# Weighted sum of gathered expert rows: from one token per partition on the full array to eight tokens per gather on column tiles

## The chip, the cores and the metric

One core of one Trainium2 chip runs the whole program. The metric is the device time of one execution in microseconds (us). PE is the matmul engine (PEld its weight loads), DVE, ACT and POOL are the vector, scalar and GpSimd engines, SP issues the plain DMAs. POOL issues the indirect DMAs, called gathers here.

## The reference, cut to what matters

Two layers (shared shape, own weights) run over a prompt block of 128 tokens and a sample of 512. Each layer is a mixer (three kinds of heads) and then PEER, a retrieval of experts, in which nearly all bytes are moved. For each block of 128 tokens and each of 8 heads:

```python
s = einsum('nhpk,pmk->nhpm', q, sub_keys)              # 2 x 128 scores
sv, si = top_k(s, 16)                                  # on each half
cand = sv[:, :, 0, :, None] + sv[:, :, 1, None, :]     # 16 x 16
top_s, top_j = top_k(cand, 16);  e = expert numbers of top_j
g = softmax(top_s)
act = gelu(einsum('nd,nhkd->nhk', x, u[e]))
y = einsum('nhk,nhkd->nd', g * act, v[e])
x = x + gate * y
```

u and v have 16384 rows of 1024 floats per layer. Per block, 8 heads x 16 picks x 128 tokens rows of u and as many of v are fetched, 4 KB each. All is float32.

## The kernel before, in words

A *unit* is one head of one block of one layer: 2 x 5 x 8 = 80 units (`UNITS`), with 16 *rows* each. Row r of u is one gather: pick number r % 16 of all 128 tokens, partition p getting the expert row of token p (512 KB). Rows of v are fetched in the same way, from the same index tile `idx_st`. There are 1280 rows of each (`ALL_ROWS`).

All engines run one list of steps in the order of `whole_order`; each takes the steps that concern it, in order, and waits on semaphores. `weave` puts mixer steps between the row steps, in proportion to rough costs, and never right after the last row of a unit. Up to row 980 (of 1280) there is mixer work between most rows; after that there are only row steps. At step r:

- POOL (`expert_row`) issues v row r - 16 into one of four v buffers, once the sum of the row four before has ended (`summed`), and then u row r + 4 into one of four u buffers, once DVE has finished u row r.
- DVE multiplies u row r with the tokens and sums it to one column of `dots` (L1863), and does one piece of the top-k of the unit two ahead (`topk`, a generator). When a unit's 16 dots are there, DVE and ACT turn them into weights (`gelu_args`, `gelu`, `weights`), 128 x 16.
- ACT makes, for v row r - 18, a diagonal 128 x 128 matrix of its weights (`diagonal`, L1376, seven buffers).
- PE sums v row r - 20 (`V_LAG`): two matmuls, left and right half, diagonal x row, accumulated in `acc` (expert_sum in the trace) over the 128 rows of a block (L2200). In the trace each of these matmuls is two records, as is every float32 matmul of the kernel; a row is four.

After a block ACT copies the sum out, DVE gates it and adds it to x (`finish`). In the last 20 rows DVE adds every second v row itself (`add_row`, `SHARED_ROWS`), and the last 16 v rows also use the four u buffers, which are free then (`v_place`).

`work` is four PSUM banks for everything else on PE; `Banks` hands them out along the plan, by `fills_of`. The scores of a unit are one matmul into such a bank (`peer_scores`), made at the last row of the unit three before.

## Time and profile before

| | |
|---|---|
| median of 3 runs | 4307.49 us (4300.9 to 4318.6) |
| span of the profiled execution | 4295.3 us, first to last instruction; what lies around it is not in the trace (12.2 us against the median) |
| PE busy | 82% of the span, mean granted clock 0.967 |
| DVE, POOL, ACT busy | 60%, 60%, 18% |
| bytes moved | 1521 MB, of which 1342 MB by gathers; mean 354 GB/s |
| L2200, the weighted sum, on PE | 5080 records, 2505.5 us busy |
| L1863, dot products, on DVE | 1280, 1557.0 us busy |
| L1079, gathers, on POOL | 2 x 1280, 1233.9 + 1219.9 us busy |
| L1376, diagonals, on ACT | 1270, 446.4 us busy |

The profile is one execution. Busy time is the time in which an engine has an instruction running; the DMA share is the mean busy share of the core's 16 DMA engines (it can come out a little over 1 in short stretches). [...] "Idle before, releaser" says how long an engine had nothing to do and what ended it, by semaphore events; "issue" is that no releaser was found, "remote" that it was none of this core's engines. Ends of matmuls are modelled.

### The profile page before, as it was taken

The page shows a single profiled execution, that of the slowest core. Times are in us where ns is not written, and L with a number is a line of the kernel's source. Part 1 is how long each engine was busy: PE and PEld are TensorE (multiplying, and loading weights), DVE is VectorE, ACT ScalarE, POOL GpSimd, SP SyncE. Part 2 cuts the span into 40 slices and gives each one's busy share as a digit, 9 for nine tenths or more (in the row PEclk, how much of TensorE's full clock was granted, in tenths as well). Part 3 has the DMA queues.
Part 4 walks back from the last instruction along what each step waited for, and adds up shares of the span by engine and source line. Part 5 has one row for each costly group of instructions (what it writes and reads, how often), then busy time and mean ns, then how long its engine had stood idle before and what let it go on. Part 6 is the DMA issues. An engine that isn't in the chain of part 4 may idle for free.

```text
span 4295.3 us, 37781 instructions
## 1 busy us (share of the span) xinstructions
PE 3531.0 (82%) x10578; PEld 1680.6 (39%) x10578; DVE 2580.9 (60%) x6691; ACT 759.0 (18%) x2324; POOL 2588.3 (60%) x2835
## 2 busy tenths in 40 slices
PE   7798999889887778887877999998888877777776
PEld 3444555444343233433422555543433422222222
DVE  2545567757665665656565555776766566666654
ACT  2112212212111121211111122221211111111110
POOL 1256456666665666766666654666666666666665
PEclk8999999999999999999999999999999999999999
DMA  7887999999999999999999899999999999999998
GB/s 278 317 288 265 339 362 358 365 387 379 348 365 382 380 355 348 349 351 370 383 379 373 296 331 338 368 358 375 385 346 370 362 368 374 367 370 372 370 370 327
DMA packets 461412, 1521.29 MB, mean 354 GB/s; under 512 B 47092, under 2 KB 67352, under 8 KB 460696
## 3 DMA queue, kind: packets, MB, share of 16 engines
q0 software_dynamic: 368640, 1342.34, 82.9%
q1 hardware_dynamic: 92156, 176.43, 11.3%
q8 instruction: 90, 1.47, 0.1%
q14 instruction: 114, 0.93, 0.1%
q10 hardware_dynamic: 412, 0.11, 0.0%
HBM read 1513.04 MB, written 5.67 MB: 354 GB/s over the span
## 4 chain that ended last, share of the span: by engine, by line
PE 37%; DMA 19%; issue 18%; POOL 18%; DVE 5%; another core or an unknown queue 3%; ACT 1%; SPq 0%; ACTq 0%; DVEq 0%; POOLq 0%
PE expert_sum L2200 20%; POOL expert_rows L1079 16%; DMA expert_rows<-in_peer_v,experts 14%; PE work L1959 4%; DMA expert_rows<-in_peer_u,experts 4%; PE work L2151 3%; PE work L2166 2%; DVE expert_rows L1863 2%; PE work L1905 2%; PE work L2095 2%; PE work L2122 1%; POOL stat_rstd L1029 1%; PE work L1934 1%; PE work L2051 1%
## 5 line engine op out<-in xcount | busy, mean ns | idle before, releaser
L2200 PE MATMUL expert_sum<-expert_rows,weight_diagonals 128*128 128x512 f32 x5080 | 2505.5, 623 | 588.9 <-DMA expert_rows<-in_peer_v,experts 446.8
L1863 DVE CUSTOM_DVE_ANT_0 expert_rows<-expert_rows,tokens 128x1024 f32<-128x1024 f32 x1280 | 1557.0, 1217 | 912.3 <-DMA expert_rows<-in_peer_u,experts 806.2
L1079 POOL DMA_INDIRECT expert_rows<-in_peer_v,experts x1280 | 1233.9, 964 | 1006.2 <-PE expert_sum L2200 566.9
L2200 PEld LDWEIGHTS expert_sum<-expert_rows,weight_diagonals 128*128 128x128 f32 x5080 | 912.8, 195 | 1848.4 <-issue 1676.7
L1079 POOL DMA_INDIRECT expert_rows<-in_peer_u,experts x1280 | 1219.9, 953 | 449.2 <-issue 358.4
L1376 ACT ACTIVATE weight_diagonals<-ident,expert_weights 128x128 f32<-128x128 f32 x1270 | 446.4, 392 | 568.7 <-PE expert_sum L2200 217.3
L1959 PE MATMUL work<-weight_ring,h_or_mixed 128*128 128x384 f32 (+3 forms) x768 | 237.3, 463 | 12.4 <-DMA weight_ring<-in_w_in 10.6
L1905 PE MATMUL work<-ident,scratch 128*128 128x128 f32 (+1 forms) x770 | 127.2, 289 | 97.9 <-DVE scratch L1479 32.1
L1959 PEld LDWEIGHTS work<-weight_ring,h_or_mixed 128*128 128x128 f32 x768 | 140.1, 193 | 115.3 <-issue 61.1
L1905 PEld LDWEIGHTS work<-ident,scratch 128*128 128x128 f32 (+1 forms) x770 | 97.7, 145 | 186.8 <-issue 86.1
L1315 ACT ACTIVATE scratch<-work,neg_max 128x640 f32<-128x640 f32 (+3 forms) x108 | 73.0, 676 | 502.2 <-DVE neg_max L1640 290.9
L1365 ACT ACTIVATE gelu_dots<-gelu_args 128x16 f32<-128x16 f32 x80 | 17.2, 216 | 809.1 <-issue 449.2
L2166 PEld LDWEIGHTS work<-h_or_mixed,weight_ring 128*128 128x128 f32 x1024 | 142.7, 194 | 37.8 <-issue 31.9
L2166 PE MATMUL work<-h_or_mixed,weight_ring 128*128 128x128 f32 (+1 forms) x1024 | 151.9, 304 | 4.9 <-DMA weight_ring<-in_peer_wq 3.8
L1026 POOL TENSOR_SCALAR stat_biased<-stat_sums 128x6 f32<-128x6 f32 (+1 forms) x82 | 17.5, 214 | 211.0 <-DVE stat_sums L1500 84.2
L1640 DVE TENSOR_REDUCE neg_max<-work 128x1 f32<-128x640 f32 (+3 forms) x120 | 76.3, 636 | 107.0 <-PE work L2095 67.9
L2151 PE MATMUL work<-weight_ring,scratch 128*128 128x512 f32 x304 | 133.6, 592 | 0.1
L1863 DVE DVE_READ_ACCUMULATOR2_ANT dots<- 128x1 f32 x1280 | 105.6, 82 | 0.0
L1500 DVE TENSOR_REDUCE stat_sums<-scratch 128x6 f32<-128x576 f32 (+1 forms) x42 | 27.6, 658 | 128.3 <-ACT scratch L1208 74.4
L1679 DVE COPY scratch<-work 128x512 f32<-128x512 f32 x20 | 13.8, 692 | 136.9 <-PE work L2151 136.9
L2151 PEld LDWEIGHTS work<-weight_ring,scratch 128*128 128x128 f32 x304 | 57.7, 190 | 73.1 <-issue 73.1
L1029 POOL TENSOR_TENSOR stat_rstd<-stat_biased,minus_half 128x6 f32<-128x6 f32 (+1 forms) x82 | 79.5, 969 | 6.8
(192 smaller groups left out, 2409.1 us busy)
## 6 DMA issues: line engine op xcount, KB each, us to landing
weight_ring<-in_w_mod SPq DMA_DIRECT2D x20, 2048.0 KB
weight_ring<-in_peer_wq SPq DMA_DIRECT2D x16, 2048.0 KB
weight_ring<-in_w_out SPq DMA_DIRECT2D x15, 2048.0 KB
expert_rows<-in_peer_u,experts POOLq DMA_INDIRECT x1280
expert_rows<-in_peer_v,experts POOLq DMA_INDIRECT x1280
weight_ring<-in_w_in SPq DMA_DIRECT2D x11, 1536.0 KB
expert_rows<-in_w_mod SPq DMA_DIRECT2D x4, 2048.0 KB, 13.7
weight_ring<-in_t_pool SPq DMA_DIRECT2D x4, 2048.0 KB
```

Of the source, the lines that this page charges most:

```text
L1029: g.tensor_tensor(stat_cols(rst, key, n), stat_cols(stp, key, n), half[:, 0:n], ALU.pow).then_inc(rstd_ready.sem, 1)
L1079: g.indirect_dma_start(buffer, None, table, bass.IndirectOffsetOnAxis(ap=idx_st[:, col:col + 1], axis=0),).then_inc(row_in, 16)
L1315: a_.activation(probs(item)[:, 0:n], src[:, 0:n], ACT.Exp, bias=nmax[:, i % 2:i % 2 + 1], accum_out=rsum[:, at:at + 1]).then_inc(banks.fre ...
L1376: a_.activation(diags[:, at * P:(at + 1) * P], ident[:, :], ACT.Copy, scale=wgt[:, col:col + 1]).then_inc(diag_ready, 1)
L1640: v_.tensor_reduce(nmax[:, i % 2:i % 2 + 1], s2[:, 0:n], AX.X, ALU.max, negate=True).then_inc(maxima.sem, 1)
L1863: v_.tensor_tensor_reduce(out=u_ring[r % U_RING], in0=u_ring[r % U_RING], in1=tokens[:, :], scale=1.0, scalar=0.0, op0=ALU.mult, op1=ALU.a ...
L1905: ins = t_.transpose(dst[0:n, j * P:(j + 1) * P], v, ident[:, :])
L1959: ins = t_.matmul(dst[:, lo:n], hT(b, kk), wt[:, kk, lo:n], start=kk == 0, stop=kk == KC - 1)
L2095: ins = t_.matmul(dst[:, col:col + m * P], lhs, tile(first, m)[lo:lo + n, :, pick, :], start=True, stop=True)
L2151: ins = t_.matmul(dst, o_T[:, kk, :], wt[:, kk, :], start=kk == 0, stop=kk == KC - 1)
L2166: ins = t_.matmul(dst[:, 0:len(blocks) * P], wt[:, kk, (h % 4) * P:(h % 4 + 1) * P], h_blocks[:, blocks[0]:blocks[-1] + 1, kk, :], start=k ...
L2200: ins = t_.matmul(acc[:, hf * 512:(hf + 1) * 512], diags[:, at * P:(at + 1) * P], v_buffer(row)[:, hf * 512:(hf + 1) * 512], start=first = ...
```

## The change

1. **What a v gather holds.** Partition p used to get pick k of token p. Now row k of a unit brings all 16 picks of eight tokens, those from 32 (k % 4) + 8 (k // 4) on: partition 16 i + m gets pick m of the i-th of them. For that the expert numbers of a unit have to be turned around between partitions: DVE spreads them into a masked 128 x 128 tile (`picked_of`), PE multiplies it with a 0/1 matrix (`of_group`) into 16 columns beside the scores of the unit two later, and DVE copies these to a new index tile `idx_v`.
2. **The weights.** The same turn for the weights: DVE makes the masked tile `pair_weights`, PE multiplies it with `of_group` at row 2 of the next unit (`pair_columns`), and DVE writes at row 3 (`SPREAD_AT`) the tile `spread` of 16 x 32 columns. ACT makes no diagonals any more.
3. **The sum.** The 16 gathers of a unit belong to 16 groups of eight tokens; four in turn (`STRIPS`) go to the four column tiles of 32. PE takes two gathers in one step, every second step, after both have landed: left half of the first, left half of the second, right half of the first, right half of the second. Each is a 128 x 32 weight against 128 x 512, and the two rows go to neighbouring column tiles. Each row counts up `summed` at its right half.
4. **Order.** `V_LAG` is 22 instead of 20: POOL issues v row r - 18 at step r, and PE sums rows r - 22 and r - 21 at even r. `weave` puts no mixer step after row 2 of a unit either. The DVE part in the last 20 rows is gone. Two more rounds of `peer_scores` follow at the end, for the turned numbers alone.
5. **Space.** The tile of the prompt's pooling matrix moves into another one and is loaded again for the second layer.

```diff
-U_RING, V_RING, DIAGS = 4, 4, 7
-V_LAG, DIAG_LAG = 20, 18
-SHARED_ROWS = ((ALL_ROWS - 20, ALL_ROWS),)
+U_RING, V_RING = 4, 4
+V_LAG, SPREAD_AT = 22, 3
+GROUPS, IN_GROUP, STRIPS, STRIP_T = 16, 8, 4, 32
...
+        def by_place(ap):
+            return ap.rearrange("p (i k) -> p i k", i=IN_GROUP)
+        def each_place(ap):
+            return ap.unsqueeze(1).broadcast_to([P, IN_GROUP, TOPK])
+        own_place = in_group[:, :].unsqueeze(2).broadcast_to([P, IN_GROUP, TOPK])
...
 POOL, expert_row:
+                    if v % TOPK == 0:
+                        pool.wait_ge(*banks.freed(("score", v // TOPK + 2)))
                     if no:
-                        pool.wait_ge(*v_done(v_turns[i][no - 1]))
+                        pool.wait_ge(*summed.done(v_turns[i][no - 1]))
-                    gather(peer_v, v_buffer(v), v_fills(v), v)
+                    gather(peer_v, idx_v, v_buffer(v), v_fills(v), v)
...
 ACT, expert_row:
-                if 0 <= r - DIAG_LAG < ALL_ROWS and not added_by_dve(r - DIAG_LAG):
-                    diagonal(r - DIAG_LAG)
...
 DVE, topk:
+                if unit >= 2:
+                    if unit >= 6:
+                        dve.wait_ge(*summed.done((unit - 5) * TOPK - 1))
+                    ins = v_.tensor_scalar(idx_v[:, of_unit(unit - 2)], bank(key)[:, IDX_AT:IDX_AT + TOPK], 0.0, None,
+                                           ALU.add)
...
+                v_.scalar_tensor_tensor(out=by_place(picked_of(unit)), in0=each_place(tk["flat"]),
+                                        scalar=float(layer * NEXP), in1=own_place, op0=ALU.add,
+                                        op1=ALU.mult).then_inc(picked_ready, 1)
...
 DVE, gelu_args and weights:
+                v_.tensor_tensor(by_place(pair_weights[:, :]), each_place(part[:, mine]), own_place,
+                                 ALU.mult).then_inc(gelu_step, 1)
...
-                v_.scalar_tensor_tensor(out=wgt[:, mine], in0=gel[:, mine], scalar=1.0, in1=part[:, mine],
-                                        op0=ALU.add, op1=ALU.mult).then_inc(weights_ready, 1)
+                v_.scalar_tensor_tensor(out=by_place(pair_weights[:, :]), in0=each_place(gel[:, mine]), scalar=1.0,
+                                        in1=by_place(pair_weights[:, :]), op0=ALU.add,
+                                        op1=ALU.mult).then_inc(weights_ready, 1)
+            def spread_weights(unit):
+                key = ("wv", unit)
+                dve.wait_ge(*banks.filled(key))
+                if unit >= 2:
+                    dve.wait_ge(*summed.done((unit - 1) * TOPK - 1))
+                dst = bass.AP(tensor=spread, offset=unit % 2 * TOPK * STRIP_T,
+                              ap=[[2 * TOPK * STRIP_T, P], [STRIPS * STRIP_T + IN_GROUP, 4], [STRIP_T, STRIPS],
+                                  [1, IN_GROUP]])
+                v_.tensor_tensor(dst, of_pair[:, :].unsqueeze(1).unsqueeze(1).broadcast_to([P, 4, STRIPS, IN_GROUP]),
+                                 bank(key)[:, 0:TOPK].rearrange("p (q j) -> p q j", q=4).unsqueeze(3).broadcast_to(
+                                     [P, 4, STRIPS, IN_GROUP]), ALU.mult).then_inc(banks.frees(key), 1)
...
 DVE, expert_row:
+                if k == SPREAD_AT and 1 <= unit <= UNITS:
+                    spread_weights(unit - 1)
-                if past >= 0 and added_by_dve(past):
-                    add_row(past)
...
 PE:
+                if unit >= 2:
+                    pe.wait_ge(places_ready, 3)
+                    pe.wait_ge(picked_ready, unit - 1)
+                    ins = t_.matmul(dst[:, IDX_AT:IDX_AT + TOPK], picked_of(unit - 2), of_group[:, :], start=True,
+                                    stop=True)
+            def pair_columns(unit):
+                key = ("wv", unit)
+                dst = empty(key)
+                pe.wait_ge(weights_ready, unit + 1)
+                t_.matmul(dst[:, 0:TOPK], pair_weights[:, :], of_group[:, :], start=True,
                           stop=True).then_inc(banks.fills(key), 1)
...
-                row = r - V_LAG
-                if 0 <= row < ALL_ROWS and not added_by_dve(row):
-                    n, first = divmod(row, BLOCK_ROWS)
+                last = r - V_LAG + 1
+                if 0 <= last < ALL_ROWS and last % 2:
+                    n, first = divmod(last - 1, BLOCK_ROWS)
+                    of, turn_no = divmod(last - 1, TOPK)
                     if first == 0 and n:
                         pe.wait_ge(sum_copied, n)
-                    pe.wait_ge(diag_ready, summed.at(row))
-                    pe.wait_ge(*v_landed(row))
-                    at = (summed.at(row) - 1) % DIAGS
+                    if turn_no == 0:
+                        pe.wait_ge(*banks.freed(("wv", of)))
+                    pe.wait_ge(*v_landed(last - 1))
+                    pe.wait_ge(*v_landed(last))
                     for hf in range(2):
-                        ins = t_.matmul(acc[:, hf * 512:(hf + 1) * 512], diags[:, at * P:(at + 1) * P],
-                                        v_buffer(row)[:, hf * 512:(hf + 1) * 512],
-                                        start=first == 0, stop=row == last_of_pe[n])
-                    ins.then_inc(summed.sem, 1)
+                        for d in range(2):
+                            strip, at = (turn_no + d) % STRIPS, (of % 2 * TOPK + turn_no + d) * STRIP_T
+                            tokens_at = slice(STRIP_T * strip, STRIP_T * (strip + 1))
+                            ins = t_.matmul(acc[tokens_at, hf * 512:(hf + 1) * 512], spread[:, at:at + STRIP_T],
+                                            v_buffer(last - 1 + d)[:, hf * 512:(hf + 1) * 512],
+                                            start=first < STRIPS, stop=first >= BLOCK_ROWS - STRIPS,
+                                            tile_position=(0, STRIP_T * strip))
+                            if hf:
+                                ins.then_inc(summed.sem, 1)
+                if k == SPREAD_AT - 1 and 1 <= unit <= UNITS:
+                    pair_columns(unit - 1)
```

## Rows read from the trace of the kernel before

**Rows 1.** Page, first part: busy us (share of span), instructions.
```profile
PE 3531.0 (82%) x10578; PEld 1680.6 (39%) x10578; DVE 2580.9 (60%) x6691; ACT 759.0 (18%) x2324; POOL 2588.3 (60%) x2835
```

**Rows 2.** Stretches, gathers alone: us, POOL busy (count), PEclk, DMA share, GB/s.
```profile
170.00:600.00 430.00, 173.84 (x179) 0.95 0.85 307
600.00:2390.00 1790.00, 1106.47 (x1158) 0.97 0.97 367
2390.00:2650.00 260.00, 112.40 (x118) 0.97 0.86 307
2650.00:3400.00 750.00, 470.14 (x491) 0.98 0.97 368
3400.00:4240.00 840.00, 562.76 (x591) 0.98 0.98 370
```

**Rows 3.** Stretches, all engines: busy (count) of PE, PEld, DVE, ACT, POOL.
```profile
170.00:600.00 430.00, 381.56 (x1445) 209.27 (x1444) 237.52 (x629) 87.33 (x251) 224.90 (x279) 0.95 0.85 307
2390.00:2650.00 260.00, 240.19 (x871) 135.59 (x870) 147.93 (x375) 56.54 (x165) 135.98 (x166) 0.97 0.86 307
3400.00:4240.00 840.00, 600.19 (x1239) 217.09 (x1238) 503.59 (x1303) 114.27 (x356) 562.76 (x591) 0.98 0.98 370
```

**Rows 4.** Stretches, the weighted sum (L2200) alone: PE, then PEld.
```profile
170.00:600.00 430.00, 150.75 (x308) 56.74 (x308) 0.95 0.85 307
2390.00:2650.00 260.00, 113.63 (x236) 43.55 (x236) 0.97 0.86 307
```

**Rows 5.** Waits, whole trace: waiter, releaser, us in total, times, longest.
```profile
POOL expert_rows L1079 <- PE expert_sum L2200: 566.9, 320, 8.4
PEld expert_sum L2200 <- ACT weight_diagonals L1376: 150.2, 127, 4.5
```

**Rows 6.** Waits of POOL, 170 to 600 us, then 2390 to 2650.
```profile
POOL expert_rows L1079 <- PE expert_sum L2200: 105.6, 38, 8.4
...
POOL expert_rows L1079 <- PE expert_sum L2200: 74.6, 30, 6.5
```

**Rows 7.** Waits of POOL in 3400 to 4240 us.
```profile
POOL expert_rows L1079 <- remote: 63.0, 25, 3.4
POOL expert_rows L1079 <- PE expert_sum L2200: 43.7, 35, 3.4
```

**Rows 8.** Timeline, POOL and PE: start, us, what, count [idle before].
```profile
3736.63 0.95 POOL L1079 DMA_INDIRECT expert_rows<-in_peer_v,experts  x1 [0.30 <-issue]
...
3742.93 1.95 PE L2200 MATMUL expert_sum<-expert_rows,weight_diagonals 128*128 128x512 f32 x4 [0.61 <-DMA expert_rows<-in_peer_v,experts]
...
3749.70 0.95 POOL L1079 DMA_INDIRECT expert_rows<-in_peer_v,experts  x1 [2.95 <-remote]
...
3755.41 5.34 PE L2200 MATMUL expert_sum<-expert_rows,weight_diagonals 128*128 128x512 f32 x8 [2.41 <-DMA expert_rows<-in_peer_v,experts]
```

**Rows 9.** Timeline of PE and POOL near the end.
```profile
4258.37 1.95 PE L2200 MATMUL expert_sum<-expert_rows,weight_diagonals 128*128 128x512 f32 x4 [2.14 <-DMA expert_rows<-in_peer_v,experts]
...
4260.59 1.31 POOL L1079 DMA_INDIRECT expert_rows<-in_peer_v,experts  x1 [1.90 <-PE expert_sum L2200]
```

**Rows 10.** Timeline, PE's weight loads at full and at low clock.
```profile
3741.30 0.19 PEld L2200 LDWEIGHTS expert_sum<-expert_rows,weight_diagonals 128*128 128x128 f32 x1 [0.24 <-issue]
...
3757.25 0.34 PEld L2200 LDWEIGHTS expert_sum<-expert_rows,weight_diagonals 128*128 128x128 f32 x1 [0.52 <-issue]
```

**Rows 11.** Table of stretches of 5 us, all engines.
```profile
4260.00:4265.00 5.00, 2.28 (x5) 0.68 (x4) 2.37 (x2) 0.80 (x2) 3.80 (x3) 1.00 0.75 247
4265.00:4270.00 5.00, 2.80 (x5) 1.14 (x6) 1.28 (x1) 0.00 (x0) 3.88 (x4) 0.74 0.93 305
4270.00:4275.00 5.00, 5.00 (x8) 1.83 (x7) 1.28 (x1) 0.00 (x0) 3.84 (x4) 0.58 0.97 327
4275.00:4280.00 5.00, 3.56 (x9) 1.30 (x8) 2.57 (x2) 0.00 (x0) 3.92 (x3) 1.00 0.98 378
```

**Rows 12.** Groups by line: busy us, mean ns of one | idle.
```profile
L1765 DVE TENSOR_TENSOR topk<-topk 128x512 f32<-128x512 f32 x80 | 54.9, 687 | 0.3
```

More of the change, by code:

```diff
@@ L56 @@
 ALL_ROWS = UNITS * TOPK
-U_RING, V_RING, DIAGS = 4, 4, 7
-V_LAG, DIAG_LAG = 20, 18
-SHARED_ROWS = ((ALL_ROWS - 20, ALL_ROWS),)
-def added_by_dve(row):
-    return row % 2 == 1 and any(a <= row < e for a, e in SHARED_ROWS)
-def shared_block(n):
-    return any(a // BLOCK_ROWS == n for a, e in SHARED_ROWS)
+U_RING, V_RING = 4, 4
+V_LAG, SPREAD_AT = 22, 3
+GROUPS, IN_GROUP, STRIPS, STRIP_T = 16, 8, 4, 32
+IDX_AT = 2 * NKEYS
 def near(n):
@@ L346, in weave @@
         out += [step]
-        if step[0] != "row" or step[1] % TOPK == TOPK - 1:
+        if step[0] != "row" or step[1] % TOPK in (SPREAD_AT - 1, TOPK - 1):
             continue
@@ L846, in v_landed @@
             return v_fills(row), 16 * (earlier + no + 1)
-        last_of_pe = [max(r for r in pe_rows if r // BLOCK_ROWS == n) for n in range(LAYERS * NB)]
-        def v_done(row):
-            return added.done(row) if added_by_dve(row) else summed.done(row)
-        def all_v_done(row):
-            last_pe = max(r for r in pe_rows if r <= row)
-            theirs = [r for r in added.no if r <= row]
-            return [summed.done(last_pe)] + ([added.done(theirs[-1])] if theirs else [])
         block = ctx.enter_context(nc.Block())
@@ L1074, in rope_keys_of, with gather @@
                 rope(("ukv", l, b))
-            def gather(table, buffer, row_in, row):
+            def gather(table, numbers, buffer, row_in, row):
                 col = row // TOPK % 4 * TOPK + row % TOPK
                 g.indirect_dma_start(buffer, None, table,
-                                     bass.IndirectOffsetOnAxis(ap=idx_st[:, col:col + 1], axis=0),
+                                     bass.IndirectOffsetOnAxis(ap=numbers[:, col:col + 1], axis=0),
                                      ).then_inc(row_in, 16)
@@ L1087, in row_u @@
                     pool.wait_ge(u_done, row - U_RING + 1)
-                gather(peer_u, u_ring[row % U_RING], u_in[row % U_RING], row)
+                gather(peer_u, idx_st, u_ring[row % U_RING], u_in[row % U_RING], row)
             def expert_row(r):
@@ L1831, in finish @@
                 v_.tensor_tensor(out, xb(b), block_sum[:, :], ALU.add).then_inc(x_updated.sem, 1)
-            def add_row(row):
-                unit, k = divmod(row, TOPK)
-                col = unit % 2 * TOPK + k
-                first = added.no.get(row - 2) is None
-                if first and row >= BLOCK_ROWS:
-                    dve.wait_ge(*x_updated.done(("fin", row // BLOCK_ROWS - 1)))
-                dve.wait_ge(weights_ready, unit + 1)
-                dve.wait_ge(*v_landed(row))
-                if first:
-                    v_.tensor_scalar(block_sum[:, :], v_buffer(row), wgt[:, col:col + 1], None,
-                                     ALU.mult).then_inc(added.sem, 1)
-                    return
-                dve.wait_ge(*added.done(row - 2))
-                v_.scalar_tensor_tensor(out=block_sum[:, :], in0=v_buffer(row), scalar=wgt[:, col:col + 1],
-                                        in1=block_sum[:, :], op0=ALU.mult, op1=ALU.add).then_inc(added.sem, 1)
             def expert_row(r):
@@ L1856, in expert_row @@
                         pass
-                    ahead[0] = topk(unit + 2) if unit + 2 < UNITS else iter(())
+                    ahead[0] = topk(unit + 2) if unit < UNITS else iter(())
                 if r < ALL_ROWS:
```

82 lines of the change are left out of this document (42 added, 40 removed).

## The prediction

> **What bounds the kernel now.** I read the page first: PE is busy for 82% of the span, DVE and POOL for 60% [rows 1]. A share over the whole span hides stages, so the second view is the table of stretches. From 170 us on, pairs of gathers (one of peer_u, one of peer_v, 1.05 MB together) run all the time. Count them by stretch [rows 2]: 179 gathers in 170 to 600 us are 89.5 pairs, 4.80 us each, with the DMA engines 85% busy; 1158 + 491 gathers in 600 to 2390 and 2650 to 3400 are 824.5 pairs in 2540 us, 3.08 us each, DMA 97%; 118 gathers in 2390 to 2650 are 59 pairs, 4.41 us each, DMA 86%; 591 in 3400 to 4240 are 295.5 pairs, 2.84 us each, DMA 98%. So there are two kinds of stretch. In the two with low DMA share PE is the full engine: 382 of 430 us and 240 of 260 us [rows 3], of which 151 and 114 us are the weighted sum [rows 4], and POOL waits there for the sum to free a v buffer, 106 and 75 us [rows 6], out of 567 us in all [rows 5]. Everywhere else the gathers themselves set the pace.
>
> The third view is why a pair takes 2.84 us in the stretch with no mixer. POOL issues a gather in 0.95 us with 0.30 us ahead of each [rows 8], so two take 2.50 us: POOL alone would allow 2.50. In 840 us it waits 63 us for something the trace calls remote and 44 us for the sum [rows 7], which is 0.36 us per pair; 2.50 + 0.36 is about the 2.84. [...]
>
> **The loop that the change touches.** There are four v buffers. A gather may start when the sum of the row four earlier is done, so before the change 4T >= L + P, with T the time of a pair of gathers, L from the start of a v gather on POOL to the start of its sum on PE, P from there to POOL's next start. L: 3736.63 to 3742.93 is 6.3 us, and 3749.70 to 3755.41, behind a pause that makes the match certain, is 5.7 us [rows 8]; I take 6.2, bounds 5.7 and 6.3. P: 4258.37 to 4260.59 is 2.2 us [rows 9]. Hence 4T >= 8.4, T >= 2.1 us: today the loop has 4 x 2.84 - 8.4 = 3.0 us to spare per four pairs, and 3.9 us where T is 3.08.
>
> **The change part by part.**
> 1. Two rows are summed at once, so neither starts before the second has landed. POOL issues v, u, v, u; the second v starts 2 x 1.25 = 2.5 us behind the first. The even row's buffer opens the loop again: 4T >= 2.5 + L + P'. This is an added wait. Queued behind it on PE are the mixer's matmuls and the next pair; POOL waits for PE, and the u gathers stand behind the v gather on POOL.
> 2. P' is the price that no row shows, since no matmul here uses a column tile. A row is now four records 0.43 us apart (0.19 load + 0.24) at full clock and 0.86 us (0.34 + 0.52) at the low level [rows 10]. If tiles overlap, two records of one tile still follow each other, and of a pair's eight records the other row's fall into the same slots: four slots per pair in a stream, and the even row is done at the fourth: P' = P = 2.2 us, 3.9 us at the low clock. If they do not overlap, the even row is done after six records: 6 x 0.43 + 0.5 = 3.1 us, low 6 x 0.86 + 0.5 = 5.7 us (0.5 is what P = 2.2 holds beyond its four records). The even row could not be done before four records, so below nothing is excluded. I take overlap, since the two tiles share neither weights nor outputs. [...]
> 3. T from the loop: at full clock (2.5 + 6.2 + 2.2) / 4 = 2.73 us; at the low clock (2.5 + 6.2 + 3.9) / 4 = 3.15 us. The spare 3.0 us that now swallow hiccups are gone, so the remote waits add their 63 us / 295.5 = 0.21 us per pair: 2.94 and 3.36 us.
> 4. Which clock? PE now runs 600 of 840 us in the last stage [rows 3] and keeps 0.98. With overlap it runs about 2.1 us in a cycle of two pairs of 5.9 us. [...] I take a third of the time at the low level (bounds none and all): T = 2/3 x 2.94 + 1/3 x 3.36 = 3.08 us against 2.84 now. 295.5 pairs x 0.24 = **+71 us** (bounds: with L = 5.7, the full clock and no remote waits T = 2.60, so 295.5 x -0.24 = -71; all at the low level 295.5 x 0.52 = +154).
> 5. The two PE-bound stretches: the sum's 151 and 114 us halve, up to 75 and 57 us less. The DMA engines can't be more than about 98% busy: 430 x 0.85 / 0.98 = 373 us and 260 x 0.86 / 0.98 = 228 us, so at most 57 and 32 us. The mixer keeps its chains of waits; I take **-45 and -25 us** (bounds 0 and -89 together).
> 6. The remaining 2540 us: PE gets lighter by up to half of the sum, which shortens the part of the 567 us of waits that lies here and at the end, 567 - 106 - 75 - 44 = 342 us. Against that the spare of the loop falls from 3.9 us to 4 x 3.08 - 10.9 = 1.4 us, and mixer blocks that PE runs between pairs meet that. I take **+30 us** (bounds -150 and +150).
> 7. The end: POOL runs v 18 rows behind instead of 16, so two more gathers of about 1.4 us come after the last u, and DVE no longer adds half of the last rows: **+7 us** (bounds 0 and +15).
> 8. At nothing: the diagonals go from ACT. PE's weight loads waited 150 us for them [rows 5], part of which comes back inside the items above, as the next late thing in both cases is the landing. DVE gains one 128x512 product per unit (0.69 us by the line of its like [rows 12]) and three 128x128 ones, a quarter of that and more each, some 1.5 us in all per 16 pairs (about 45 us), in the 40% in which it idles; uncovered it would be 80 x 1.5 = 120 us. Once per unit DVE now waits for a small PE product at row 3 and PE for the weights at row 2. Behind DVE's wait stand the next dot products, and POOL's u gathers wait for those; four u buffers cover it, and if not, it costs a PE block of up to 7 us now and then. The 160 small matmuls add some 0.5 us of PE each, 80 us, at places where PE now has room. The reloaded pooling matrix is 0.26 MB once.
>
> Sum: 71 - 45 - 25 + 30 + 7 = +38 us. The profiled execution's span is 4295.3 us, 12.2 us under the median of 4307.5; these 12 us lie around the span and stay. Forecast 4345 us, **0.9% slower**; its own range is 4310 to 4400.
>
> **The rivals.**
> - *PE's relief wins (faster).* Place: all stretches with mixer. Price: -70 us in item 5, -20 in item 6, the last stage even, +7 at the end: -83, 4225 us. It holds if the clock stays high and if the remote waits become shorter with fewer gathers in flight, so that T stays at or under 2.84; with these gains it turns into a loss once T in the last stage passes 2.84 + 83 / 295.5 = 3.12 us. For it: POOL's 567 us of waits for PE. Against: only 181 of them lie where the DMA engines have room.
> - *The tiles do not overlap.* Then T is (2.5 + 6.2 + 3.1) / 4 + 0.21 = 3.16 us in the last stage, +0.32 x 295.5 = +95 us; item 5 gives nothing; in item 6 the spare is 12.3 - 11.8 = 0.5 us and PE is as full as before, +0.13 x 824.5 = +107; with the end +210: 4520 us. For it: each record's rows show strict order on PE. This is also the case that the change does not do what it says.
> - *The clock stays at the low level* in the last stage and much of the middle: +154 there, +0.1 x 824.5 = +82, item 5 halved to -35, +7: +208, 4515 us. For it: the two stretches of [rows 11]; against it: the next 5 us there are back at 1.00.
>
> **How the numbers follow.** Forecast 0.45; relief wins 0.30; no overlap 0.15; low clock 0.10. I leave a tenth on either side: the low end takes in the relief case, 4225, the high end stops short of the last two, 4500. Runs of this kernel agree within about 0.4%, so 0.5% (21 us) is what can be told from no change. Faster by more than that: the relief case, 0.30, and a little of the forecast's low side, 0.01, is 0.31. Within: 0.14, all from the forecast's low side. Slower: 0.55.
>
> **What would show it.** Item 1: L + 2.5 + P' near 4T in the last stage, and POOL's waits for the sum well over 44 us there. Item 2: in the records of one pair, the second row's first record starting beside the first row's second; then PE's sum falls from 2506 us toward 1300 to 1700. Item 4: PEclk in the last stage near 0.8 and T near 3.1. Item 5: DMA share over 0.9 in the two early stages and mixer steps ending sooner. Wrong if the last stage keeps 2.84 us per pair, or if the clock stays at 0.98 with PE idle for two thirds of it.

## The result, and the profile after

The changed kernel takes 4652.1 us (median of 4 runs, 4642.8 to 4664.4); the kernel before takes 4313.1 us beside it (4 runs, 4300.9 to 4323.6). The ratio is 1.079, interval 1.077 to 1.081: 7.9% slower. The forecast was 4345 us, with 4500 us as the high end of the range. The direction was right, the size was not, and the time lies outside the range.

The page of the changed kernel, beside [rows 1]: the span (4662.5 us against 4295.3), the first part, the granted clock in 40 slices (PEclk, in tenths of the full one), and the groups (busy us, mean ns of one | idle before, releaser) of the sum, its weight loads and the v gathers.

```profile
span 4662.5 us, 37150 instructions
...
PE 3069.7 (66%) x10938; PEld 1218.0 (26%) x10938; DVE 2624.5 (56%) x7003; ACT 365.4 (8%) x1055; POOL 2578.3 (55%) x2836
...
PEclk8889878787777778877867988878777866667667
...
L2214 PE MATMUL expert_sum<-expert_rows,weight_columns 128*32 128x512 f32 x5120 | 1781.6, 834 | 1370.4 <-DMA expert_rows<-in_peer_v,pair_experts 1340.3
...
L1078 POOL DMA_INDIRECT expert_rows<-in_peer_v,pair_experts x1280 | 1225.4, 957 | 1239.3 <-PE expert_sum L2214 942.2
...
L2214 PEld LDWEIGHTS expert_sum<-expert_rows,weight_columns 128*32 128x32 f32 x5120 | 343.4, 134 | 2376.7 <-issue 2368.6
```

No engine is full any more. PE fell from 82% to 66% of the span, and its weighted sum from 2505.5 to 1781.6 us. But PE now idles 1340 us for landings (447 us before), and POOL idles 942 us for the sum, where it idled 567 us [rows 5]. Two engines that wait for each other form a loop: gather, landing, sum, free buffer, next gather.

All engines by stretch (us, then busy (count) of PE, PEld, DVE, ACT, POOL, then the granted clock as a share of the full one, DMA share, GB/s), to be held against [rows 2, 3]:

```profile
170.00:600.00 430.00, 352.38 (x1518) 186.87 (x1517) 243.46 (x675) 64.44 (x176) 216.07 (x270) 0.90 0.82 295
600.00:2560.00 1960.00, 1255.68 (x4319) 472.87 (x4318) 1143.10 (x3070) 136.07 (x406) 1140.02 (x1232) 0.77 0.93 335
2560.00:2870.00 310.00, 254.34 (x1039) 128.50 (x1038) 175.27 (x459) 43.44 (x119) 161.30 (x193) 0.88 0.87 312
2870.00:3710.00 840.00, 563.42 (x2126) 238.87 (x2124) 516.66 (x1353) 68.28 (x192) 482.13 (x509) 0.80 0.92 332
3710.00:4600.00 890.00, 476.51 (x1258) 111.37 (x1256) 495.10 (x1327) 12.34 (x52) 536.10 (x565) 0.69 0.93 335
```

In the long stretches the DMA share went from 0.97 and 0.98 to 0.93 and 0.92, and the bytes per second fell with it, in the last stage from 370 to 335 GB/s: the DMA engines get fewer gathers per us than they served before. The clock, 0.97 before, is 0.77 to 0.80 in the middle and 0.69 at the end.

The loop itself can be read off a timeline of the last stage, to be held against [rows 8, 9]:

```profile
3999.94 0.94 POOL L1078 DMA_INDIRECT expert_rows<-in_peer_v,pair_experts  x1 [2.31 <-PE expert_sum L2214]
...
4002.43 0.94 POOL L1078 DMA_INDIRECT expert_rows<-in_peer_v,pair_experts  x1 [0.30 <-issue]
...
4005.66 0.94 POOL L1078 DMA_INDIRECT expert_rows<-in_peer_v,pair_experts  x1 [1.03 <-PE expert_sum L2214]
...
4008.50 0.21 PEld L2214 LDWEIGHTS expert_sum<-expert_rows,weight_columns 128*32 128x32 f32 x4 [4.81 <-issue]
4008.53 3.20 PE L2214 MATMUL expert_sum<-expert_rows,weight_columns 128*32 128x512 f32 x8 [3.11 <-DMA expert_rows<-in_peer_v,pair_experts]
4009.36 0.21 PEld L2214 LDWEIGHTS expert_sum<-expert_rows,weight_columns 128*32 128x32 f32 x2 [0.64 <-issue]
...
4011.98 0.94 POOL L1078 DMA_INDIRECT expert_rows<-in_peer_v,pair_experts  x1 [1.63 <-PE expert_sum L2214]
...
4014.03 1.91 PE L2214 MATMUL expert_sum<-expert_rows,weight_columns 128*32 128x512 f32 x8 [1.54 <-DMA expert_rows<-in_peer_v,pair_experts]
```

The even row's gather starts at 3999.94 and the odd one's at 4002.43, 2.49 us later. The pair's sum starts at 4008.53, 6.10 us after the odd gather. The even buffer is gathered into again at 4011.98, 3.45 us after that. Together 12.04 us for four pairs of gathers, 3.01 each. POOL waited for the sum each time it came to an even row (2.31, 1.03 and 1.63 us). The eight records took 3.20 us mostly at the low clock, and 1.91 us in the next pair at the full one.

The same stretch in steps of 1 us (PE busy, clock, DMA share, GB/s):

```profile
4009.00:4010.00 1.00, 1.00 (x4) 0.50 1.01 348
4010.00:4011.00 1.00, 1.00 (x4) 0.50 0.91 303
4011.00:4012.00 1.00, 1.00 (x6) 0.92 0.99 393
4012.00:4013.00 1.00, 0.48 (x4) 1.00 1.00 393
```

The granted clock is 0.50 here (the traces show two levels, 0.50 and 1.00) while the pair is summed, and reaches 1.00 only when the sum, at work since 4008.53, is nearly done.

**Where the 367 us of the two profiled spans lie.** The start times of the u gathers in the two traces give the time per pair of gathers (one u, one v) for any stretch of rows, and this is the unit in which I compare everything below. "no mixer" is the last stage.

```
rows of u       0-92  92-340 340-408 408-592 592-664 664-734 734-980 980-1279 (no mixer)
before, us      4.41   3.07    3.00    3.19    2.90    4.34    3.07    2.84
after, us       4.45   3.39    3.31    3.50    3.17    4.45    3.37    3.15
added, us        +4     +78     +21     +55     +20      +8     +75     +91
```

The first u gather came 10.6 us later (169.4 and 180.0 us), and what follows the last one took 4.9 us more. The sum is +367.

### The profile page after: what moved, and what is told of

It reads as the page before. It is cut to its first block, busy times and chain, and to the rows that moved or that the text cites. A ratio compares the mean times of both kernels' runs of the same rounds, so it can differ in the third digit from the quotient of the medians.

```text
span 4662.5 us, 37150 instructions
## 1 busy us (share of the span) xinstructions
PE 3069.7 (66%) x10938; PEld 1218.0 (26%) x10938; DVE 2624.5 (56%) x7003; ACT 365.4 (8%) x1055; POOL 2578.3 (55%) x2836
## 4 chain that ended last, share of the span: by engine, by line
DMA 31%; PE 27%; issue 19%; POOL 16%; DVE 4%; ACT 1%; another core or an unknown queue 1%; SPq 0%; ACTq 0%; POOLq 0%; DVEq 0%
DMA expert_rows<-in_peer_v,pair_experts 26%; PE expert_sum L2214 16%; POOL expert_rows L1078 15%; DMA expert_rows<-in_peer_u,experts 3%; PE work L1955 2%; PE work L2147 2%; DVE expert_rows L1865 2%; PE work L2091 1%; PE work L1901 1%; PE work L2118 1%; PE work L2162 1%; PE work L1930 1%; DMA weight_ring<-in_w_mod 1%; POOL stat_rstd L1028 1%
## 5 line engine op out<-in xcount | busy, mean ns | idle before, releaser
L2214 PE MATMUL expert_sum<-expert_rows,weight_columns 128*32 128x512 f32 x5120 | 1781.6, 834 | 1370.4 <-DMA expert_rows<-in_peer_v,pair_experts 1340.3
L1078 POOL DMA_INDIRECT expert_rows<-in_peer_v,pair_experts x1280 | 1225.4, 957 | 1239.3 <-PE expert_sum L2214 942.2
L2214 PEld LDWEIGHTS expert_sum<-expert_rows,weight_columns 128*32 128x32 f32 x5120 | 343.4, 134 | 2376.7 <-issue 2368.6
L1955 PE MATMUL work<-weight_ring,h_or_mixed 128*128 128x384 f32 (+3 forms) x768 | 249.3, 481 | 9.5 <-DMA weight_ring<-in_w_in 5.9
L1901 PE MATMUL work<-ident,scratch 128*128 128x128 f32 (+1 forms) x770 | 147.6, 320 | 116.9 <-DVE scratch L1471 42.6
L2162 PE MATMUL work<-h_or_mixed,weight_ring 128*128 128x128 f32 (+1 forms) x1024 | 167.4, 324 | 9.7 <-DVE h_or_mixed L1483 4.2
L1360 ACT ACTIVATE topk<-topk 128x16 f32<-128x16 f32 x80 | 24.3, 304 | 844.6 <-DVE topk L1747 771.1
L2091 PE MATMUL work<-mla_qkv_or_x_and_queries 96*128 96x512 f32 x192 | 76.7, 532 | 6.7 <-DVE weight_columns L1835 3.1
```

The source lines that it names most:

```text
L1078: g.indirect_dma_start(buffer, None, table, bass.IndirectOffsetOnAxis(ap=numbers[:, col:col + 1], axis=0),).then_inc(row_in, 16)
L1901: ins = t_.transpose(dst[0:n, j * P:(j + 1) * P], v, ident[:, :])
L1955: ins = t_.matmul(dst[:, lo:n], hT(b, kk), wt[:, kk, lo:n], start=kk == 0, stop=kk == KC - 1)
L2091: ins = t_.matmul(dst[:, col:col + m * P], lhs, tile(first, m)[lo:lo + n, :, pick, :], start=True, stop=True)
L2162: ins = t_.matmul(dst[:, 0:len(blocks) * P], wt[:, kk, (h % 4) * P:(h % 4 + 1) * P], h_blocks[:, blocks[0]:blocks[-1] + 1, kk, :], start=k ...
L2214: ins = t_.matmul(acc[tokens_at, hf * 512:(hf + 1) * 512], spread[:, at:at + STRIP_T], v_buffer(last - 1 + d)[:, hf * 512:(hf + 1) * 512], ...
```

## The experiments

They ran on three chips of the same kind, here called chips 0, 7 and 9. On chip 0: each gather summed by itself, the pair's wait alone, the zeros, and v, v, u, u. On chip 9: the two kernels, V_LAG 20, and three buffers. On chip 7: v, v, u, u with zeros, the order of the halves, and five buffers. The kernel before takes 4119.7, 4119.9 and 4120.8 us on chips 0, 7 and 9 (not 4313), so their runs can be compared with each other. The kernel after takes on chip 9 nearly what it took at first; "the first chip" is that of the section above. Ratios are always to the kernel before on that same chip.

**The two kernels there.**

> The kernel before, unchanged, for a profile on the same chip as the others of this call. All theories: the same time as the kernel before, and stretches as in its first profile, scaled by the chip's DMA rate.

> The changed kernel, unchanged, beside the kernel before on this chip. Ratio 1.07 to 1.09 as in its first measurement; in the stretch with no mixer about 0.3 us per pair of gathers over the kernel before, with the clock at 0.7.

Measured: 4119.7 us (one run) and 4636.8 us, ratio 1.126 (1.122 to 1.129), above the 1.07 to 1.09 that was expected. The stage without mixer, 800 us of each, before and after:

```profile
3267.00:4067.00 800.00, 621.79 (x1338) 228.91 (x1336) 525.02 (x1357) 119.03 (x369) 583.53 (x616) 1.00 1.02 405
...
3710.00:4510.00 800.00, 434.55 (x1142) 99.70 (x1138) 454.78 (x1222) 11.50 (x48) 485.26 (x510) 0.68 0.94 336
```

The kernel before moves 405 GB/s here, where it moved 370 on the first chip [rows 3], and this goes with a time that is 4.5% shorter. POOL's remote waits, 145 us in the kernel before on the first chip, are gone as well. The kernel after gained only 0.3% (4652 to 4637 us) and stays at 336 GB/s. So its time isn't set by the transfer rate; that it is set by the loop is what the next runs test.

**Column tiles and turned numbers, but no waiting for a pair.** The kernel after with each gather summed by itself:

```diff
-                    pe.wait_ge(*v_landed(last - 1))
-                    pe.wait_ge(*v_landed(last))
+                    pe.wait_ge(*v_landed(row))
...
                     for hf in range(2):
-                        for d in range(2):
-                            strip, at = (turn_no + d) % STRIPS, (of % 2 * TOPK + turn_no + d) * STRIP_T
...
```

> The changed kernel with one edit: PE sums each gather alone as soon as it has landed, in its own column tile, at every step; V_LAG stays 22, turned numbers and weights stay. Theory A (the wait for a pair, and the low clock that goes with it, cost the 339 us): the loop is 4T >= L + P again, PE has its 1.7 us per row back and its clock returns to about 0.97, the stretch without mixer goes from 3.15 to about 2.84 us per pair of gathers, the whole to 4270 to 4350 us. Rival B (the turning of numbers and weights through PE and DVE once per unit, or switches between tile modes, cost it): those are all still there, so 4550 us or more.

> The changed kernel with each gather summed alone and V_LAG back at 20. Theory A: as with V_LAG 22, ratio to the kernel before about 1.01, at most 0.2% less, since v gathers end two steps earlier behind the last u. Rival F (the two steps of extra lag hold back the start of every block and the end): 1% less, ratio at or under 1.00.

Measured: 4169.3 us, ratio 1.011 (1.008 to 1.014). With V_LAG 20 in place of 22: 4159.8 us, 1.009 (1.007 to 1.012). The sum's group and the last stage:

```profile
L2212 PE MATMUL expert_sum<-expert_rows,weight_columns 128*32 128x512 f32 x5120 | 2289.5, 617 | 520.8 <-DMA expert_rows<-in_peer_v,pair_experts 513.5
```
```profile
3317.00:4117.00 800.00, 611.93 (x1407) 138.56 (x1406) 536.30 (x1424) 14.40 (x60) 582.10 (x616) 1.00 1.02 405
```

Both lines are of the run with V_LAG 22. So the new gathers, the extra DVE and PE products, the narrower weights and the missing diagonals together cost 1%, most of it in the stretches with mixer (2.99 us per pair against 2.94). The last stage stays at 2.60 us. V_LAG costs nearly nothing. Of the 12.6%, 11.5 points belong to the step from here to the kernel after: the pair, with the clock that it brings.

**The pair's wait, but no column tiles.** The kernel before, made to wait for both rows and then to sum them row after row on the full array. It also waits for both diagonals, and has V_LAG 22 and no DVE part in the last 20 rows, as the kernel after:

```diff
-                    pe.wait_ge(*v_landed(row))
+                    pe.wait_ge(*v_landed(last - 1))
+                    pe.wait_ge(*v_landed(last))
+                    for row in (last - 1, last):
...
```

> The kernel before with one edit: PE waits for two landed gathers and then sums them row after row with full 128-column diagonals at every second step (V_LAG 22; the DVE part in the last 20 rows is off). No turning, no column tile. Theory A: the even row adds the 2.5 us between two v gathers to the loop while P stays 2.2 us at full clock: (2.5 + 6.2 + 2.2)/4 + 0.21 = 2.94 us per pair in the last stage, 0.1 to 0.2 us more over 1280 pairs, 4440 to 4570 us; the clock stays above 0.9. Rival B: 4313 us as before, within 1%.

Measured: 4572.3 us, ratio 1.107 (1.102 to 1.111), spread 4543 to 4602. The last stage came as expected (2.95 us per pair of gathers, 2.94 written). The stretches with mixer cost about 0.4 us per pair, where 0.1 to 0.2 was written.

```profile
L2202 PE MATMUL expert_sum<-expert_rows,weight_diagonals 128*128 128x512 f32 x5120 | 2602.8, 658 | 764.1 <-DMA expert_rows<-in_peer_v,experts 740.2
```
```profile
3750.00:4550.00 800.00, 578.05 (x1147) 231.52 (x1146) 461.68 (x1192) 114.50 (x324) 515.34 (x543) 0.91 0.96 357
```

Waiting for the pair and summing it in one go makes most of the loss, without any column tile and with a clock of 0.92 over the run. With mixer a pair of gathers takes 3.37 and 3.32 us (rows 92 to 340, 734 to 980), as much as the kernel after needs (3.36 and 3.32). Only in the last stage is the kernel after worse: 3.13 against 2.95 us.

**The clock.** The kernel after, with two matmuls on zeros after every pair, which keep PE busy and add nothing:

```diff
+                    if STRIPS <= first < BLOCK_ROWS - STRIPS:
+                        for hf in range(2):
+                            t_.matmul(acc[:, hf * 512:(hf + 1) * 512], ident[:, :],
+                                      zeros[:, :].unsqueeze(1).broadcast_to([P, 64, 8]), start=False, stop=False)
```

> The changed kernel with PE work added that does not change the sum: after each pair (but for the first and last four rows of a block) two matmuls of the identity with a zero moving operand, 128x128 by 512 columns, accumulated into the same banks; four records, 1.7 us at full clock. Theory A with the clock as a large part: PEclk rises from 0.78 to over 0.9, P' falls from up to 3.9 to 2.2 us, which is about 0.25 us per pair where the clock was low, 4380 to 4500 us in all although PE has 1088 us more work. Rival C (only the wait counts, the clock does not): 4650 us or more.

Measured: 4562.3 us, ratio 1.109 (1.105 to 1.113), where 4380 to 4500 us was expected. The sum, the added matmuls, and the last stage:

```profile
L2216 PE MATMUL expert_sum<-expert_rows,weight_columns 128*32 128x512 f32 x5120 | 1366.9, 658 | 706.1 <-DMA expert_rows<-in_peer_v,pair_experts 703.5
...
L2224 PE MATMUL expert_sum<-zero_rows,ident 128*128 128x512 f32 x2400 | 1235.5, 637 | 0.0
```
```profile
3707.00:4507.00 800.00, 569.60 (x1796) 181.21 (x1796) 493.43 (x1309) 12.12 (x51) 538.81 (x567) 0.96 0.98 373
```

1235 us of useless work make the kernel 74 us faster. In the last stage the clock is 0.96 in place of 0.68, and the sum over the whole run falls from 1768 (kernel after on chip 9) to 1367 us. By stretch (table below) 91 us are gained without mixer (299 pairs, 3.13 to 2.82 us) and 29 us in rows 340 to 408 and 592 to 664; 44 us are lost in rows 0 to 92 and 664 to 734, where PE is fullest; in the long stretches with mixer nothing is gained (3.36 and 3.36; 3.32 and 3.37).

**A shorter wait for the pair.** The kernel after with POOL's order v, v, u, u in place of v, u, v, u, so that the two gathers of a pair are issued back to back:

```diff
-                v = r - V_LAG + V_RING
-                if 0 <= v < ALL_ROWS:
+                for v in ((r - V_LAG + V_RING, r - V_LAG + V_RING + 1) if r % 2 == 0 else ()):
+                    if not 0 <= v < ALL_ROWS:
+                        continue
```

> The changed kernel with the order of POOL's gathers changed: at even steps both v gathers of a pair back to back, then u; at odd steps u alone. The second v starts 1.25 us behind the first, not 2.5. Theory A: 1.25 us less in the loop of four rows, 0.31 us per pair of gathers, if the loop is what limits: 4250 to 4400 us. Rival B or D (the DMA queues or the turning limit): within 1% of 4652 us.

Measured: 4303.2 us, ratio 1.044 (1.042 to 1.046). This order of issue takes back 334 of the 517 us. The distance of the two gathers falls from 2.55 to 1.27 us, and a pair of gathers takes 3.11 and 3.10 us with mixer, 2.76 without. POOL's wait for the sum over the whole run (us in total, times, longest), first in the kernel after on chip 9, then here:

```profile
POOL expert_rows L1078 <- PE expert_sum L2214: 925.8, 424, 12.4
```
```profile
POOL expert_rows L1078 <- PE expert_sum L2215: 598.7, 362, 12.2
```

**Both, where the clock is low.** The same order, and the two zero matmuls from u row 980 on:

> The kernel with the gathers issued in the order v, v, u, u (ratio 1.044), and two zero matmuls of 512 columns after each pair's sum, from u row 980 on alone (the last stretch, without mixer). Theory (in the last stretch the low clock lengthens the sum and with it the loop): 2.76 us per pair of gathers there fall to about 2.60, some 48 us in all, ratio 1.03. Rival (with the pair's wait short the clock no longer matters): 1.044.

Measured: 4264.3 us, ratio 1.034 (1.031 to 1.038). The last stage without and with them:

```profile
3442.00:4242.00 800.00, 460.73 (x1284) 106.88 (x1280) 495.06 (x1343) 12.34 (x52) 549.93 (x579) 0.71 1.00 381
```
```profile
3411.00:4211.00 800.00, 603.53 (x1928) 194.94 (x1923) 520.36 (x1415) 13.33 (x56) 576.51 (x608) 0.97 1.02 400
```

The clock goes from 0.71 to 0.97, 2.76 us per pair of gathers to 2.63, 39 us in all (expected were 48), and the last stage is then 0.03 us per pair above the kernel before, where the kernel after was 0.53 above it. So the pair's distance and the clock together are nearly the whole loss of that stage. Of the 144 us that still separate this run from the kernel before, about 128 lie in the stretches with mixer, and were not taken apart further.

**The order of the halves.** The kernel after with both halves of the first row ahead of both of the second:

```diff
-                    for hf in range(2):
-                        for d in range(2):
+                    for d in range(2):
+                        for hf in range(2):
```

> The kernel after with the sums of the two rows of a pair one after the other (both halves of the first, then both of the second) in place of the left halves of both first. Theory (the loop of gather, wait for the pair and the sum of its first buffer sets the time): the first row's own two halves take the four places after which its buffer was free before, so it becomes free as early as in the kernel after, the second one later by up to three places; the ratio to the kernel before is between 1.12 and 1.15 (the kernel after had 1.126). Rival (left halves first is what frees the buffers late): the time falls by 2% or more, to 1.10 or less.

Measured: 4629.7 us, ratio 1.124 (1.121 to 1.128), the same as the kernel after within both intervals. "Left halves first" is neither gain nor loss here. The expectation that the second row is done up to three places later is not borne out. In the pair of the line below the eight records start at 0, 13, 428, 467, 857, 896, 1285 and 1325 ns, and the last record of each row (the one that counts up `summed`) is the seventh and the eighth. So here too the records of the two rows run side by side, though all of the first row's were issued ahead of the second's, and the pair takes 1.92 us as against 1.91 in the kernel after:

```profile
4011.90 1.92 PE L2214 MATMUL expert_sum<-expert_rows,weight_columns 128*32 128x512 f32 x8 [1.43 <-DMA expert_rows<-in_peer_v,pair_experts]
```

**How long is the loop?** The kernel before with three v buffers, and with five (POOL then issues v row r - 17, or r - 15, at step r, in place of r - 16):

```diff
-U_RING, V_RING, DIAGS = 4, 4, 7
+U_RING, V_RING, DIAGS = 4, 3, 7
```

> The kernel before with one v buffer less (V_RING 3) and nothing else. Theory A (the loop of v buffers sets the pace once it has no spare): one step of four goes, about the same loss of lead as the pair wait (2.5 us of 11.3): 3T >= 8.4 + hiccups, about 3.0 us per pair, ratio 1.05 to 1.11. Rival E (the pair wait costs by PE doing two rows in one go, so that the buffers come back in bursts, and not by the lost lead): ratio under 1.03.

```diff
-U_RING, V_RING, DIAGS = 4, 4, 7
+U_RING, V_RING, DIAGS = 4, 5, 4
...
-        mpp = sb("prompt_pooling", 4 * P)
+        mpp = ML[:, 8064:8064 + 4 * P]
```

The fifth buffer is paid for with three of the seven buffers for diagonals, and with the pooling matrix, which is loaded again for the second layer.

> The kernel before with five buffers for the gathers in place of four (the pooling constant that does not fit beside them is loaded again for the second layer). Theory (the loop gather, sum, free buffer is what limits the gathers, and the kernel before has little spare in it): five periods instead of four cover the loop, the stretches with mixer fall from 2.92 us per pair of gathers to about 2.8, the last stretch stays at 2.60, so ratio 0.97 to 0.99. Rival (the queue of POOL and the memory already set the pace of the kernel before, and only the kernel after is limited by the loop): no change, 1.00 within 0.005.

Measured: three buffers 4440.9 us, 1.077 (1.073 to 1.080); five 4071.9 us, 0.988 (0.986 to 0.991). POOL's wait for the sum with three, with four (the kernel before), with five:

```profile
POOL expert_rows L1079 <- PE expert_sum L2200: 1040.0, 895, 8.3
```
```profile
POOL expert_rows L1079 <- PE expert_sum L2200: 624.5, 590, 8.2
```
```profile
POOL expert_rows L1081 <- PE expert_sum L2202: 370.7, 235, 8.2
```

With three buffers the loop has no spare without mixer (in rows 990 to 1240 POOL waited for the sum at 235 of 250 v gathers), and its length can be read: 3 x 2.81 = 8.4 us, which is the 8.4 us of the prediction (mean 6.13 from gather to sum, 2.25 from there to the next gather). With mixer it is 3 x 3.24 = 9.7 us (7.1 and 2.6); there POOL waited for the sum at 138 of 220 v gathers (rows 750 to 970), so 9.7 us is a mean that holds some other waits too. The lead that one buffer less takes away (one period, 2.6 to 3.1 us) is no smaller than the pair's distance, but it costs 7.7% and the pair's wait 10.7%: the lost lead is most of the pair's price and not all of it. The fifth buffer makes a kernel that beats both, by 1.2%: 2.94 to 2.87 us in rows 92 to 340, 3.12 to 2.99 in rows 408 to 592, 2.92 to 2.89 in rows 734 to 980, and nothing in the last stage (2.60), where the loop wasn't the limit. The gain with mixer is about half of what was expected (2.8 us); with four diagonals in place of seven PE's weight loads wait 488 us for them (313 in the kernel before), and what this takes from the gain was not tested.

Per pair of gathers, on the chip of each run (before and after on chip 9):

```
rows of u           0-92  92-340 340-408 408-592 592-664 664-734 734-980 980-1279
before              4.40   2.94    2.91    3.12    2.72    4.35    2.92    2.60
after               4.46   3.36    3.33    3.45    3.16    4.36    3.32    3.13
single              4.40   2.99    2.91    3.13    2.69    4.42    3.00    2.60
pair, no tiles      4.66   3.37    3.13    3.49    3.11    4.61    3.32    2.95
after + zeros       4.72   3.36    3.16    3.49    2.93    4.64    3.37    2.82
v, v, u, u          4.43   3.11    3.12    3.25    2.81    4.12    3.10    2.76
same + zeros at end 4.50   3.07    3.05    3.28    2.83    4.15    3.13    2.63
before, 3 buffers   4.56   3.24    3.09    3.42    2.85    4.50    3.24    2.81
before, 5 buffers   4.36   2.87    2.91    2.99    2.69    4.35    2.89    2.60
```

## Why the prediction was right in direction and wrong in size

Four periods are the pair's distance, plus L, plus P', by the way the three are cut. So the sum alone proves nothing; what shows that the loop sets the pace is that POOL waited for the sum at 83 of the 125 gathers that begin a pair (rows 990 to 1240 of the kernel after, first chip), and the runs above. The means over the stretches, read from the starts of the gathers and sums in each trace:

```
                      distance   L      P'    sum / 4
after, with mixer       2.56    7.34   3.69    3.40    (rows 100-330, first chip)
pair, no tiles, mixer   2.57    7.71   3.28    3.39    (rows 100-330, chip 0)
after, no mixer         2.52    6.38   3.70    3.15    (rows 990-1240, first chip)
after + zeros, no mixer 2.51    6.32   2.47    2.83    (rows 990-1240, chip 0)
v, v, u, u, no mixer    1.26    6.21   3.63    2.77    (rows 990-1240, chip 0)
```

- *Item 1, the wait:* right. Distance 2.5 us as forecast; POOL waits for the sum 207 us in 3710 to 4600 where it waited 44 [rows 7]:

```profile
POOL expert_rows L1078 <- PE expert_sum L2214: 206.9, 96, 4.0
```

- *Item 2, overlap:* right, and with it the rival "the tiles do not overlap" falls. At the full clock eight records take 1.91 us where four on the full array took 1.95 [rows 8, 9]; at the low clock two weight loads of a pair start 0.86 us apart (4008.50 and 4009.36). P' at the low clock was put at 3.9 us, at the full one at 2.2; the run with zeros shows 2.47. Two tiles so give 2 x 1.95 / 1.91 = 2.04 times. The sum was put at 1300 to 1700 us; it is 1782 at the clock that it got, and 1367 with the zeros, at a mean clock of 0.93.
- *Item 3, the hiccups:* wrong, and by luck with little effect, since its 62 us (0.21 x 295.5) made up for most of what item 4 had too low. The 0.21 us for remote waits did not come: among POOL's waits in the last stage there is no remote one, and in the whole run there is one of 2.0 us, where the kernel before had 145 us. What these waits stood for, and why they went, no trace here shows.
- *Item 4, the clock:* right in kind, too small. I took a third of the time at the low level. That was my estimate, and no run shows it: a mean clock of 0.69 is 62% of it ((1 - 0.69) / 0.5). And what counts is the clock while a pair is summed: in rows 990 to 1240 the mean granted clock during the pairs' sums is 0.63, and in 78% of the pairs it is under 0.75, which goes with a mean P' of 3.70, between the 2.2 and 3.9 of the forecast. Measured +91 us where +71 was written; with the hiccups of item 3 and the low level throughout the sum would have given +154. The rival "the clock stays low" came nearer to the level (all of the time, measured 62%) and had the wrong sum, +208 us, since it priced the middle at +0.1 us per pair.
- *Item 5, the two stretches bound by PE:* wrong. -70 us was written, +11 came. PE's sum did fall, from 151 us [rows 4] to 83 in 170 to 600, and POOL's wait from 106 us [rows 6] to 75, but a pair of gathers takes as long as before. The 98% that I took as the most the DMA engines can be busy was the highest share in [rows 2]; on chip 9 it was 1.02. The sum alone in the two stretches:

```profile
170.00:600.00 430.00, 83.35 (x280) 16.31 (x280) 0.90 0.82 295
...
2560.00:2870.00 310.00, 83.97 (x280) 16.01 (x280) 0.88 0.87 312
```

  The table of all runs tells two things apart. The wait alone costs 4.40 to 4.66 us in rows 0 to 92 and 4.35 to 4.61 in 664 to 734, +42 us. The halved sum (pair, no tiles, against after) gives back 4.66 to 4.46 and 4.61 to 4.36, -36 us. So the relief came, at half of its forecast size, and the pair's wait, which I had charged in the other stretches alone, took all of it. With the short wait the relief shows in rows 664 to 734 (4.12), and not in rows 0 to 92 (4.43); what sets those was not isolated.
- *Item 6, the rest of the mixer's stretches: this is the step that failed.* +30 us for 824.5 pairs was written, 0.04 us each; measured +249 us, 0.30 each, beyond even its upper bound of +150. It took the loop of the last stage at the full clock, 2.5 + 8.4 = 10.9 us, for stretches where L and P' are longer, and so found a spare of 4 x 3.08 - 10.9 = 1.4 us. Measured are 2.56 + 7.34 + 3.69 = 13.6 us, 3.40 us per pair of gathers: 1.3 us more than four of the old periods in place of 1.4 us less. The run with three buffers shows that the loop was longer there before the change too, 9.7 us in place of 8.4, so an estimate of the old spare is 4 x 3.08 - 9.7 = 2.6 us and not 3.9, hardly more than the 2.5 us of the added wait. That alone would use up the spare and still not slow the gathers: 9.7 + 2.5 = 12.2 us, 3.05 us each. The remaining 1.4 us came with summing the pair in one go. In the kernel after they stand mostly in P' (3.69 in place of 2.6 us), while PE's clock is 0.77; in the run without tiles, with as long a loop, half of them stand in L (7.71 in place of 7.1 to 7.2) and half in P' (3.28), at a clock of 0.92. So the low clock is not needed for them. How they divide between PE's order of mixer steps and pairs, the burst of two rows and the clock stays open.
- *Item 7:* +7 us written, +5 measured after the last u gather.
- *Item 8, at nothing:* small, but not nothing: the run without the pair's wait costs 1.1%, 50 us that I had priced at zero (against the 80 us of small products that had been seen and put where PE has room; in the kernel after they are 63 us of PE). Which part of it (turned numbers, small matmuls, the changes between full array and column tiles) was not separated.

Against the sum of +38 us, the 329 us that are missing are +219 from item 6, +81 from item 5, +20 from item 4, -2 from item 7, and 10.6 us by which the gathers began later, which the later runs show in one (178.5 us in the kernel after, chip 9) and not in another (171.2 us with the other order of halves, chip 7) and which I leave unexplained.

The rival "PE's relief wins" fell because relief is worth little to a loop that consists of transfer latency and waiting: 36 us in the two PE-heavy stretches, and elsewhere nothing. The halved sum did not shorten P', since the even row's four records follow each other in any case (1.91 us for the pair, 1.95 for one row before), and the clock fell (0.967 to 0.78 over the run).

One more thing stays open in item 6: with mixer the zeros bring P' down from 3.65 to 3.20 us but raise L from 7.38 to 7.77, and the time stays. Whether the low clock costs anything there could not be told apart from what the added matmuls cost.

## What to carry to other kernels

In a ring of buffers compare the whole loop (issue, latency, wait for partners, work, release) with the number of buffers times the period, and measure the loop in each kind of stretch; a run with one buffer less gives its length where the loop then sets the pace. Work that consumes two transfers at once adds their distance to that loop (2.5 us here, 1.3 with the two back to back), so issue them back to back or add a buffer before merging them. Before halving an engine's work, ask how much of the time that engine's work ends the wait: here only in two short stretches, and its clock fell along with its load (0.98 to 0.69 in the last stage), which there lengthened the work inside the loop (P' was 3.70 us, and 2.47 with the zeros).

## What the runs showed of the hardware

- Two float32 matmuls on neighbouring column tiles of 32 ran side by side: eight records of 512 columns in 1.91 us at the full clock, against four in 1.95 us on the full array. They did so in either order of issue (1.92 us with all of the first row's ahead of the second's).
- Between a full-array matmul and one on a column tile the next one started 93 ns later than behind one of the same kind: 522 ns in place of 429 behind 512 columns, 415 in place of 322 behind 384, and 202 in place of 109 behind 128, all at the full clock. Going from the column tile to the full array was seen behind 512 columns alone, with the same 522. What PE does in these 93 ns the trace does not show. In the run without pairs there are 627 changes each way, which by an estimate (1254 x 93 ns) is 117 us of PE in 4169; what of that reaches the time was not separated.
- With the lighter load the granted clock was lower for whole stages. Last stage: 0.69 with PE at work 477 of 890 us (kernel after), 0.96 with 570 of 800 (with zeros), 1.00 with 622 of 800 (kernel before). The added work on zeros bought 0.31 us per pair of gathers.
- Chips of one kind moved 370 GB/s (the first) and 405 GB/s (chip 9) in the last stage for the same instructions: the kernel before takes 4.5% less time there, the kernel after 0.3% less. Whether the chip or something beside it made the difference is not known.
